# The order of the query tiles in the attention of a two-layer transformer trunk, one core of Trainium2

## What is computed

```python
rel = relu(einsum('bqhd,bsd->bqhs', qib, ki))
score = einsum('bqh,bqhs->bqs', wib, rel)
score = where(pos[None, :] <= t[:, None], score, NEG_INF)
_, sel = top_k(score, 256)                      # the 256 best keys of a query
s = einsum('bqhd,bqkd->bhqk', qb, k[sel])
o = einsum('bhqk,bqkd->bqhd', masked_softmax(s, sel <= t), v[sel])
```

## Time and profile before

| what | value |
|---|---|
| three runs, us | 3994.72, 4007.64, 4033.19 |
| median, us | 4007.64 |
| profiled execution, us | 4022.36 |
| its span, us | 4020.6 |
| TensorE busy / VectorE / ScalarE / GpSimd, us | 3323.2 / 2157.9 / 1339.0 / 833.6 |
| mean granted TensorE clock | 0.896 |
| attention of layer 0, us from the start | 215 to 1042 |
| attention of layer 1, us from the start | 2476 to 3012 |

### The profile page before, as it was taken

One profiled execution on the slowest core, in us unless ns is written; L12 is line 12 of the kernel. 1 busy time (PEld: TensorE's weight loads), 2 busy tenths in 40 slices (PEclk: granted clock), 3 DMA queues, 4 the chain that ended last, 5 costly groups with the idle time before them and its releaser, 6 DMA issues. The chain is left out here.

```text
span 4020.6 us, 50943 instructions
## 1 busy us (share of the span) xinstructions
PE 3323.2 (83%) x16860; PEld 2711.5 (67%) x16860; DVE 2157.9 (54%) x3679; ACT 1339.0 (33%) x2797; POOL 833.6 (21%) x661
## 2 busy tenths in 40 slices
PE   7888999999969999999775402888889699999995
PEld 5777888888747777777544302666667477777774
DVE  5455555555156555555555697444440755455555
ACT  4255444545233121212234442444441322121221
POOL 2300000000143322323231000010102432322322
PEclk8699889989989999999988756989899899999998
DMA  4100000002201111111020000000022011111111
GB/s 148 42 1 18 16 16 16 16 16 95 84 26 42 42 47 37 52 42 49 19 76 11 10 0 0 16 31 16 31 105 84 22 53 47 42 47 37 52 37 42
DMA packets 165578, 159.04 MB, mean 40 GB/s; under 512 B 6037, under 2 KB 149079, under 8 KB 164951
## 3 DMA queue, kind: packets, MB, share of 16 engines
q1 hardware_dynamic: 165463, 157.67, 12.1%
HBM read 128.29 MB, written 27.26 MB: 39 GB/s over the span
## 5 line engine op out<-in xcount | busy, mean ns | idle before, releaser
L373 PE MATMUL PS<-HH,WH 128*128 128x512 f32 x2160 | 883.0, 409 | 83.5 <-DVE HL L490 43.7
L374 PE MATMUL PS<-HL,WH 128*128 128x512 f32 x2160 | 861.5, 399 | 0.0
L375 PE MATMUL PS<-HH,WL 128*128 128x512 f32 x2160 | 859.3, 398 | 0.0
L373 PEld LDWEIGHTS PS<-HH,WH 128*128 128x128 f32 x2160 | 419.1, 194 | 172.5 <-issue 90.3
L375 PEld LDWEIGHTS PS<-HH,WL 128*128 128x128 f32 x2160 | 418.0, 193 | 90.5
L374 PEld LDWEIGHTS PS<-HL,WH 128*128 128x128 f32 x2160 | 419.3, 194 | 79.9
L362 POOL TENSOR_TENSOR WL<-WR,WH 128x1024 fp32r<-128x1024 f32 x187 | 457.7, 2448 | 15.6
L358 POOL TENSOR_TENSOR TOUCH<-WR 128x1 f32<-128x1 f32 x187 | 42.7, 228 | 1593.5 <-PE PS L375 874.2
L595 PE MATMUL PS<-m_KDH,m_QS 128*128 128x512 f32 (+2 forms) x192 | 93.6, 488 | 247.6 <-ACT m_PX L785 197.9
L1117 ACT ACTIVATE U_c<-PS 128x512 f32<-128x512 f32 x88 | 52.8, 600 | 490.3 <-PE PS L375 474.2
L595 PEld LDWEIGHTS PS<-m_KDH,m_QS 128*128 128x128 f32 x192 | 42.6, 222 | 255.0 <-ACT m_PX L785 213.8
(11 more groups left out here) (330 smaller groups left out, 6988.5 us busy)
## 6 DMA issues: line engine op xcount, KB each, us to landing
WR<-in_ffn_w_up SPq DMA_DIRECT2D x88, 512.0 KB, 3.8
WR<-in_ffn_w_down SPq DMA_DIRECT2D x44, 512.0 KB, 3.5
WR<-in_dsa_w_in SPq DMA_DIRECT2D x16, 512.0 KB, 4.7
WR<-in_nsa_w_in SPq DMA_DIRECT2D x15, 512.0 KB, 5.2
HH<-oh_save SPq DMA_DIRECT2D x2, 3584.0 KB, 12.3
HL<-ol_save SPq DMA_DIRECT2D x2, 3584.0 KB, 20.8
XN<-in_x SPq DMA_DIRECT2D x8, 512.0 KB, 7.0
x_save<-XT_a SPq DMA_DIRECT2D x1, 4096.0 KB, 13.3
```

The costliest lines, as they stand in the source:

```text
L373: nc.tensor.matmul(dst, wh, xh, start=start, stop=False)
L374: nc.tensor.matmul(dst, wh, xl, start=False, stop=False)
L375: return nc.tensor.matmul(dst, wl, xh, start=False, stop=stop)
```

## The change

The tiles of a pair are taken in the order 3, 0, 2, 1, 7, 4, 6, 5. `PLACE[i]` is the place of tile i in that order, and everything that counts tiles now counts places: semaphore values, the slot of `ON`, and the first tile's wait for the save. Tile i's queries, masks, gates and the place of its output in `OTH` and `OTL` still go by i. Because tile 3 needs the indexer's mask, TensorE in layer 1 waits, behind the first projection and ahead of unit 0, for a new semaphore that VectorE raises when all mask tiles are written.

```diff
+TILE_ORDER = (3, 0, 2, 1, 7, 4, 6, 5)
+PLACE = {i: n for n, i in enumerate(TILE_ORDER)}
@@ attention_plan
-    for i in range(QT):
+    for i in TILE_ORDER:
@@ transposes_pe
-                    pe.wait_ge(a.ob, m * 2 * QT + 2 * i + 2)
-                    last = nc.tensor.transpose(PS[:, b, 0:P], a.B["ON"][:, i % 2, :], IDENT[:, :])
+                    pe.wait_ge(a.ob, m * 2 * QT + 2 * PLACE[i] + 2)
+                    last = nc.tensor.transpose(PS[:, b, 0:P], a.B["ON"][:, PLACE[i] % 2, :], IDENT[:, :])
@@ output_pe, exp_act
-            t = 2 * i + h
+            t = 2 * PLACE[i] + h
@@ pair_act
-                        if item[1] == 0:
+                        if PLACE[item[1]] == 0:
@@ gates_dve
-            i, h, d, e = t // 2, t % 2, t % 2, t % 4
+            i, h, d, e = TILE_ORDER[t // 2], t % 2, t % 2, t % 4
@@ combine_dve
-            i, h, d = t // 2, t % 2, t % 2
+            n, h, d = t // 2, t % 2, t % 2
-            on = B["ON"][:, i % 2, h * DH:(h + 1) * DH]
+            on = B["ON"][:, n % 2, h * DH:(h + 1) * DH]
@@ pair_dve
-                        dve.wait_ge(a.oth, m * QT + item[1] + 1)
-                        if item[1] == 0:
+                        dve.wait_ge(a.oth, m * QT + PLACE[item[1]] + 1)
+                        if PLACE[item[1]] == 0:
@@ attention_pe
             qproj_half(pe, a, 0, 0, 0, 0, DT, first=True)
+            if a.nb == 1:
+                pe.wait_ge(sem1["mask"], 1)
             for u in range(2):
                 scores_pe(pe, a, 0, u)
@@ prep1_dve, behind the loop over the mask's tiles
+            dve.sem_inc(S["mask"], 1)
```

More of the change, by code:

```diff
@@ L1534, in trunk @@
             "wh", "wl", "ch", "cl", "kv", "chain", "zero", "rot", "t1", "qhi", "qlo", "sc", "rel",
-            "acc", "cand", "sgn")}
+            "acc", "cand", "sgn", "mask")}
         def prep1_loads(sp):
```

## The result

The change is slower: 4071.08 us as the median of four runs (4053.41 to 4074.49) against 4016.2 us for four runs of the kernel before on the same chip (3994.72 to 4033.19). The ratio is 1.0131, with a 95% interval of 1.007 to 1.0191, so some 53 us (28 to 77; the medians lie 55 apart). The forecast was +25.5 us, 4033 us; 4071.08 lies in the range, but the cost is twice the forecast.

A forecast was written before the change was run, and what follows sets the result against it. TensorE (83% busy) was taken to bound layer 0 nearly alone, and layer 1 with 92 us idle. Terms 8 + 10 + 4.5 + 3 = 25.5 us on the 4007.6 us median gave 4033 us; range 3985 to 4085.

The forecast's parts named there:

- mechanism of cover: TensorE's work is conserved; what is moved out from under the query chain comes back as waiting.
- half-clock rival: Layer 0's steps 8 to 15 thin, so clock falls and tile 7 runs at 1.2 GHz: 4062 to 4095 us; chance 0.28.
- The clock, taken at +3 us: Layer 0: more and longer waits in steps 8 to 15 bring slow stretches oftener, +3 us, bounds -52 to +65.
- Layer 1's pair, +1.0 forecast: Layer 1: each pair 1.0 us longer, +8 for eight; upper bound +2.7 with one more half-clock stretch (1.7 us).
- The steps up to the end of the second projection: Layer 1 pair: first projection ends 1.8 us later, second half's first unit 1.5, second projection's end 2.85.
- The chain: Layer 1's query path over ACT, POOL and DVE, 9.0 us: taken to shrink by 0.3 us, at most 1.7.
- steps 12 to 14 hold tile 5 for tile 7, -1.35: Layer 1 pair: lighter steps before the next pair give back 1.35 us, so its unit 0 starts 1.5 us late.
- The entry, +4.5: Layer 1's start, once: 12 matmuls queue behind the mask wait before step 1; +4.5 us, within +2.2 to +5.3.
- Layer 0, +10: Layer 0: +0.7 us after the rotation and +0.5 in steps 12 to 15, +1.2 a pair, +10 for eight; bounds 0 to 23.
- the wait for line 900 behind the rotation: Layer 0 sign: TensorE's wait there for an output tile's copy from PSUM, 1.39 us before, grows to about 2 us.
- Cover by the heavy unit: Layer 1: heavy tile 7 fills both query waits, 3966 us; chance 0.11 together with a luckier clock.
- Nothing moves: Chains shrink as much as cover, layer 0 stays TensorE-bound; only the mask's 4.5 us remain, 4012 us; chance 0.19.

The follow-up runs named there:

- l1_only: New order in layer 1 alone, with the mask wait; layer 0 in order 0 to 7: 4052.69 us, ratio 1.0062 to the kernel before.
- wait_only: Kernel before, order 0 to 7 in both layers, with only the mask wait added ahead of layer 1's first scores: 4038.8 us in one run.
- fill_old: Kernel before, order 0 to 7, with unread matmuls (14 and 6) ahead of layer 1's two query waits: 3989.88 us, ratio 0.9937.
- early_old: Kernel before, order 0 to 7, layer 1's half projections in two steps instead of four, rotation two steps earlier: 4002.08 us, ratio 0.9959.
- l0_only: New order in layer 0 alone; layer 1 in order 0 to 7 without the mask wait: 4037.74 us, ratio 1.0039 to the kernel before.
- fill_new: The change with unread matmuls (15 and 6) ahead of layer 1's two query waits: 4044.12 us, ratio 1.0069 to the kernel before.
- early_new: The change with layer 1's half projections in two steps instead of four, rotation two steps earlier: 4023.21 us, ratio 1.0018 to the kernel before.
- second_half: Kernel before with order 0, 1, 2, 3, 7, 4, 6, 5 in both layers, no mask wait: 4038.27 us in one execution.
- fill_all_old: Kernel before, order 0 to 7, with unread matmuls ahead of the larger TensorE waits of both layers: 3953.44 us, ratio 0.9847.
- fill_all_new: The change, mask wait included, with unread matmuls ahead of the larger TensorE waits of both layers: 3978.59 us, ratio 0.9898 to the kernel before.
- first_half: Kernel before with order 3, 0, 2, 1, 4, 5, 6, 7 in both layers and the mask wait: 4048.53 us in one run.

## Why the prediction was right and wrong

The forecast named the side and the mechanism of cover, and its terms without the clock, 8 + 10 + 4.5 = 22.5 us, are nearly what the whole order costs at a held clock, 25.1 us. By layers they fit less well: 10 against 9.4 in layer 0, but 12.5 against 18.9 in layer 1. What was mis-sized most is the term that stood last and smallest. That 4071.08 lies in the range is owed to the half-clock rival, for whose sake the range went up to 4085, and not to the sum.

*The clock, taken at +3 us: the term that was mis-sized.* By the profiles attention grew by 50.0 us (20.8 + 29.2), and at a held clock by 28.3 (9.4 + 18.9). The rest, 21.7 us, is what filling takes away: the clock in the main, and in layer 0 perhaps also waits put down to issue, 9.4 us more in the change's profile than in before's (14.8 for 5.4) and alike in the two filled kernels (six each). By the medians the rest is 55 - 25 = 30. In layer 1 a pair grew by 3.4 us, 2.1 of them at a held clock, so some 1.35 by the clock; by PE's busy time it is up to 2.4, and the runs leave it between the two. As a check, between the levels 1 and 0.5, a mean of 0.86 over 71.7 us is 20 us at the lower one (2 x 0.14 x 71.7), and 0.90 over 68.25 us is 14. In layer 0, unfilled, five profiles with the old order there (before, l1_only, wait_only, fill_old, early_old) have a mean of 825.3 us, and four with the new (the change, l0_only, fill_new, early_new) 845.3 us: 20 us, of which 9.4 are the order's and up to 5.5 waits put down to issue (a mean of 15.9 us a profile for 10.4). The prediction worked out the clock for layer 0 alone, from pairs that differ in the earlier trace rows; it read the 0.90 of layer 1 in the earlier trace rows and gave it no term in the sum, only a bound: one more stretch at the lower level, 1.7 us. The pairs of layer 1 in before have one period, 68.25 us; with a clock of 0.90 in each that shows only that the clock falls in every pair alike. A measure of the gap is what the held clock is worth in before itself: 68.25 - 62.53 = 5.7 us a pair.

The rule of the Trainium skill that the prediction weighed ("TensorE: Matmul & The Clock Gate", section "Terms": half of the throttled time is lost) agrees with second_half: its pair has 30 us at the lower level, before's has 14, and half of the difference is 8 us where 7 were measured. For the change's pair the same working gives 3 us of its 3.4, of which 2.1 are there at a held clock too; as a price of the clock alone it is thus an upper bound. The same page's section "A second HAM failure mode: psum-queue depth-cycling" tells of a kernel in which frequent micro-idles between groups of matmuls made the clock swing. The runs with filled waits agree, in kernels of float32: over the pairs of layer 1 the clock is 0.90 in before, 0.95 in fill_old with the two longest waits filled, and 1.00 in fill_all_old with short ones filled too. It is what I should have weighed, because it reaches short waits.

*Layer 1's pair, +1.0 forecast, +2.1 at a held clock.* The steps up to the end of the second projection are right to 0.3 us. The chain did not shrink (0.3 forecast, 0 measured). The step that failed is "steps 12 to 14 hold tile 5 for tile 7, -1.35": they gave back 0.55 (2.85 to 2.3). In fill_all_new 0.67 us of the difference stands at the filling, which waits 1.00 us in place of 0.33 for the rotation, so part of this may be the experiment's own. Another 0.6 is the wait for an exponential (1.1 us for 0.5), which grew as much without the filling. Unfilled, the same waits grew by 1.0 us a pair, which is the forecast's figure.

*The entry, +4.5.* Measured +4.6 in the change, and +3.1 in wait_only with its smaller tiles.

*Layer 0, +10.* The size is right, 9.4 at a held clock, the place is not: the wait for line 900 behind the rotation did not grow. How the 1.2 us a pair split over its steps is left open.

*The rivals.* Cover by the heavy unit (3966 us) falls: both query waits are there. "Nothing moves" (4012) falls. The half clock was told as all or nothing, in layer 0 and from the fifth fallen pair on; what happened is that mechanism in small, in both layers, on top of the forecast. It was due as a term of the sum, not only as a rival.

## What to carry to other kernels

When an edit leaves the instructions as they are and moves them, compare busy time and granted clock stretch by stretch before reading waits: equal waits gave pairs of 68.25 and 75.2 us. To tell what an order costs by itself, fill the bound engine's waits in both kernels and compare at a held clock. Work that stands beside a latency chain is its cover; moved out, it comes back as waiting, and a share of it again as lost clock. Filling only some of the waits can mislead: fill_new and fill_old lie as far apart as the unfilled kernels. Filling nearly all with work of no use beat the kernel before by about 1.5% (0.9847, interval 0.9787 to 0.9907), and is worth a run where TensorE's waits are short and many.

## What the runs showed of the hardware that I had not expected

- Matmuls whose result nobody reads make the kernel faster. Twenty a pair in layer 1 gave 27 us, those over both layers some 61 to 65 us (3953.44 against 4018.55, 3952.38 against 4013.39). They seem to steady it too: four runs of fill_all_old lie within 6.2 us, nine of fill_all_new within 18.4, twelve of before beside them within 54.
- The clock's answer to the same loop body need not be the same each time: 67.8 and 72.2 us in turn in first_half, 65.8 and 70.8 in fill_new. What decides which pair falls these runs don't show.
- A wait put down to issue at the first projection matmul of a pair in layer 0 comes once in before's loop (5.4 us), three times in the change (14.8 us in all) and in six pairs of fill_all_old:

```profile
PE PS L376 <- issue: 23.6, 6, 4.1
```

No run tried what sets it off, but the profiles show what goes with it. The transfers of the queue that is of the kind "instruction", over the whole of before and of the change (count, MB, share of the 16 engines):

```profile
q8 instruction: 53, 0.87, 0.1%
q8 instruction: 71, 1.16, 0.1%
```

Kernels with one, two, three, four and six such waits have 53, 62, 71, 80 and 98 or 99 transfers, and in every run they lie in the pairs that wait: 8 to 10 in each of these, none or one in a pair that does not. I read this as some passes of the loop having their instructions fetched again and others not; the ones that do start 3.7 to 5.4 us late. In fill_all_old that is 3.9 us in each of six pairs, still to be had if the fetching can be avoided. Why one pass fetches and the next does not is left open.
